# A fused two-block transformer layer on one core: inverse roots in 9 operations, half-empty weight tiles split only where they hold columns, and the compression blocks of the keys built earlier

## The reference

```python
# every norm of both blocks
y = xf * lax.rsqrt(jnp.mean(xf * xf, axis=-1, keepdims=True) + eps)

# second block: one projection gives everything
hn = rms_norm_2(h, attn_pre_norm)
proj = hn @ w_in
(q_n, k_c, v_c, k_s, v_s, k_w, v_w, g_n, q_w, k_sw, v_sw) = jnp.split(proj, IN_SPLITS, axis=-1)
# widths: q_n 512, six of 128, g_n 24, q_w 512, k_sw 128, v_sw 128

def compress(kv, pe, w1, w2):                 # for keys and for values
    ch = kv.reshape(B, S // 16, 16, H, D)
    blocks = jnp.concatenate([ch[:, :-1], ch[:, 1:]], axis=2) + pe[None, None, :, None, :]
    flat = blocks.transpose(0, 1, 3, 2, 4).reshape(B, nc, H, 32 * D)
    return jax.nn.gelu(flat @ w1) @ w2        # nc = 15 blocks, H = 2 heads, D = 64

# then: compressed, selected and windowed attention, mixed by sigmoid(g_n), and beside them
# a sliding-window attention (q_w, k_sw, v_sw) with sinks; both normed and projected by w_out
```

## Time and profile before

| | us |
|---|---|
| median of 3 runs | 1259.17 (1258.34 to 1260.98) |
| the profiled execution | 1257.46 |
| its span, first to last instruction | 1255.7 |
| TensorE busy | 1185.2 (94%) |
| VectorE busy | 904.7 (72%) |
| ScalarE busy | 606.6 (48%) |
| DMA | 197.51 MB, mean 157 GB/s |
| mean granted TensorE clock | 0.978 of 2.4 GHz |

### The profile page before, as it was taken

How to read it: one execution, slowest core, us unless ns; L and a number is a source line. 1 busy time by engine, 2 the same in 40 slices (tenths; PEclk the granted TensorE clock), 3 DMA queues, 4 the chain that set the end, 5 groups by cost and what they waited for, 6 DMA issues and landing times.

```text
span 1255.7 us, 24116 instructions
## 1 busy us (share of the span) xinstructions
PE 1185.2 (94%) x9174; PEld 1128.2 (90%) x9174; DVE 904.7 (72%) x1532; ACT 606.6 (48%) x1032; POOL 69.0 (5%) x56
## 2 busy tenths in 40 slices
PE   8999999999999999998999999999978897999996
PEld 8988898999999999778899999999966597999996
DVE  6999876676666596556757666557887658999855
ACT  5754654544445434344444444544455634665541
POOL 1576000000000000000000000000000000000000
PEclk9999999999999999999999999999988997999998
DMA  7454342445555556125415455555642013454552
GB/s 272 169 181 154 135 168 101 139 168 197 170 195 171 201 179 229 45 70 177 169 60 196 170 187 181 201 181 192 215 143 101 35 34 105 168 196 167 200 203 67
DMA packets 32456, 197.51 MB, mean 157 GB/s; under 512 B 3712, under 2 KB 7936, under 8 KB 9472
## 3 DMA queue, kind: packets, MB, share of 16 engines
q1 hardware_dynamic: 30752, 194.14, 44.9%
q10 hardware_dynamic: 1632, 2.36, 0.5%
HBM read 193.08 MB, written 1.05 MB: 155 GB/s over the span
## 4 chain that ended last, share of the span: by engine, by line
PE 78%; DVE 14%; ACT 4%; issue 3%; DMA 1%; ACTq 0%; DVEq 0%; SPq 0%
PE acc L486 20%; PE acc L488 20%; PE acc L487 20%; PE acc L522 7%; DVE wlo L1393 3%; DVE wlo L1386 2%; PE acc L502 2%; PE acc L787 2%; ACT whi L984 1%; PE sc L751 1%; PE st L635 1%; DMA raw<-weights 1%; DVE mx L1734 1%; PE tp L776 1%; PE tp L486 1%
## 5 line engine op out<-in xcount | busy, mean ns | idle before, releaser
L486 PE MATMUL acc<-Hhi,whi 128*128 128x256 f32 x1376 | 391.6, 285 | 3.6 <-DVE wlo L1393 3.4
L487 PE MATMUL acc<-Hlo,whi 128*128 128x256 f32 x1376 | 389.3, 283 | 0.0
L488 PE MATMUL acc<-Hhi,wlo 128*128 128x256 f32 x1376 | 389.3, 283 | 0.0
L984 ACT ACTIVATE whi<-raw 128x1024 fp32r<-128x1024 f32 x161 | 170.0, 1056 | 338.6 <-PE acc L488 312.3
L1386 DVE TENSOR_TENSOR wlo<-raw,whi 128x1024 fp32r<-128x1024 f32 x162 | 199.9, 1234 | 106.9 <-ACT whi L984 104.4
L486 PEld LDWEIGHTS acc<-Hhi,whi 128*128 128x128 f32 x1376 | 264.1, 192 | 5.0 <-DVE wlo L1393 2.3
L487 PEld LDWEIGHTS acc<-Hlo,whi 128*128 128x128 f32 x1376 | 264.1, 192 | 0.2
L488 PEld LDWEIGHTS acc<-Hhi,wlo 128*128 128x128 f32 x1376 | 264.1, 192 | 0.0
L486 PE MATMUL acc<-FH,whi 128*128 128x256 f32 x784 | 223.0, 284 | 8.3 <-DVE wlo L1393 4.5
L488 PE MATMUL acc<-FH,wlo 128*128 128x256 f32 x784 | 220.7, 281 | 0.0
L1393 DVE TENSOR_TENSOR wlo<-raw,whi 128x1024 fp32r<-128x1024 f32 x162 | 200.2, 1236 | 1.3
(11 more groups left out here) (336 smaller groups left out, 1853.4 us busy)
## 6 DMA issues: line engine op xcount, KB each, us to landing
raw<-weights SPq DMA_DIRECT2D x177, 1024.0 KB, 4.9
MEM<-mem_in SPq DMA_DIRECT2D x2, 1024.0 KB, 7.5
held<-weights SPq DMA_DIRECT2D x2, 1024.0 KB, 5.8
E<-A ACTq DMA_DIRECT2D x14, 128.0 KB, 2.3
X<-x_in SPq DMA_DIRECT2D x4, 256.0 KB, 3.5
raw<-weights SPq DMA_DIRECT2D x2, 512.0 KB, 8.1
out<-X SPq DMA_DIRECT2D x4, 256.0 KB, 2.1
cst<-consts SPq DMA_DIRECT2D x1, 998.0 KB, 12.4
```

The costliest lines, as they stand in the source:

```text
L486: pe.matmul(dst, w, x, start=first, stop=False)
L487: pe.matmul(dst, w, xl, start=False, stop=False)
L488: return pe.matmul(dst, wl, x, start=False, stop=last)
L984: act.activation(whi[j][:, 0:HALF, :], raw[j][:, 0:HALF, :], ACT.Copy).then_inc(hi_out, 1)
```

## The change

Three things. First, `inverse_root` takes 9 operations: mean plus eps as before; one multiply-add on the bits, read and written as integers; one Newton-like step with other constants; and one step of third order, as four operations. The buffer `nwi` goes. Second, `SWA_KEYS` and `SWA_VALUES` name the two tiles with zero columns: ScalarE and VectorE split only the first 128 and 152 columns of each chunk, TensorE makes only output half m = 0 of the first and products with 152 moving columns for the second, and copy, partners and rotation of the keys are one chunk wide. Third, the blocks of the keys are built ahead of rotation 6 and tile 7's product, on VectorE and ScalarE; `window_rest(0)` moves ahead of `ahead("win", 0, 8, 7)` and the values; TensorE's wait ahead of the attention is taken out, and the first `hidden_part` waits for one result fewer.

```diff
+GUESS_SLOPE, GUESS_TOP = 0.703952253, 0.703952253 * 2.38924456
+CUBIC_SCALE = 0.375 ** 0.5
...
+SWA_KEYS, SWA_VALUES = T0["win"] + 6, T0["winv"]
+WIDTHS = {SWA_KEYS: P, SWA_VALUES: P + 24}
...
+        def rot_chunks(name, k):
+            return 1 if T0[name] + k == SWA_KEYS else 2
...
                     if turned:
-                        mm = three(dst, x[:, o], xl[:, o], w, wl, a, z)
+                        n = slice(0, width)
+                        mm = three(dst[:, n], x[:, o], xl[:, o], w[:, n], wl[:, n], a, z)
...
-                turns = NTILES[name] // 2
+                turns = NTILES[name] // 2 - (name == "win")
...
             stage("win", Hhi, Hlo, source="down1", norm_name="pre2")
+            tile_in(L0["win"] + 6)
+            pe.wait_ge(acc_free, G0["win"] + 7)
+            columns(0, Hhi, Hlo, 0).then_inc(tile_done, 1)
+            tile_in(L0["win"] + 7)
+            pe.wait_ge(acc_free, G0["win"] + 8)
+            for m in range(2):
+                mm = columns(1, Hhi, Hlo, m)
+            mm.then_inc(tile_done, 1)
             to_tokens("pre2")
             tile_in(L0["winv"])
             pe.wait_ge(acc_free, G0["winv"] + 1)
             for m in range(2):
-                mm = columns(0, Hhi, Hlo, m, turned=True)
+                mm = columns(0, Hhi, Hlo, m, turned=True, width=WIDTHS[SWA_VALUES])
...
                     if kv:
                         pe.wait_ge(mix_out, 1)
+                    else:
+                        pe.wait_ge(acc_free, G0["win"] + 8 + 2)
...
-            pe.wait_ge(acc_free, G0["attn_nsa"] + 2)
             attention("attn_nsa", {5: turn_hidden, 7: compressed, 8: lambda: pe.wait_ge(cmp_ready, 1),
...
-                act.activation(whi[j][:, 0:HALF, :], raw[j][:, 0:HALF, :], ACT.Copy).then_inc(hi_out, 1)
+                act.activation(whi[j][:, 0:HALF, 0:width], raw[j][:, 0:HALF, 0:width], ACT.Copy).then_inc(hi_out, 1)
...
                     for j in range(2):
+                        if name == "win" and 2 * i + j == 7:
+                            window_blocks(0)
...
-                ins = dve.tensor_tensor(out=wlo[j][:, 0:HALF, :], in0=raw[j][:, 0:HALF, :], in1=f(whi[j][:, 0:HALF, :]),
+                ins = dve.tensor_tensor(out=wlo[j][:, 0:HALF, n], in0=raw[j][:, 0:HALF, n], in1=f(whi[j][:, 0:HALF, n]),
                                         op=ALU.subtract)
...
-                link(dve.tensor_scalar(nwi[:, 0:n], v.bitcast(I32), 1, None, op0=ALU.logical_shift_right))
-                link(dve.tensor_scalar(y.bitcast(I32), nwi[:, 0:n], -1, 0x5F3759DF, op0=ALU.mult, op1=ALU.add))
-                for step in range(3):
-                    link(dve.scalar_tensor_tensor(out=a, in0=y, scalar=-0.5, in1=v, op0=ALU.mult, op1=ALU.mult))
-                    link(dve.tensor_tensor(out=a, in0=a, in1=y, op=ALU.mult))
-                    ins = dve.scalar_tensor_tensor(out=y if step < 2 else dst, in0=a, scalar=1.5, in1=y, op0=ALU.add, op1=ALU.mult)
...
+                link(dve.tensor_scalar(y.bitcast(I32), v.bitcast(I32), -0.5, float(0x5F1FFFF9), op0=ALU.mult, op1=ALU.add))
+                link(dve.scalar_tensor_tensor(out=a, in0=y, scalar=-GUESS_SLOPE, in1=v, op0=ALU.mult, op1=ALU.mult))
+                link(dve.tensor_tensor(out=a, in0=a, in1=y, op=ALU.mult))
+                link(dve.scalar_tensor_tensor(out=y, in0=a, scalar=GUESS_TOP, in1=y, op0=ALU.add, op1=ALU.mult))
+                if between:
+                    between()
+                link(dve.scalar_tensor_tensor(out=a, in0=y, scalar=CUBIC_SCALE, in1=v, op0=ALU.mult, op1=ALU.mult))
+                link(dve.tensor_tensor(out=a, in0=a, in1=y, op=ALU.mult))
+                link(dve.scalar_tensor_tensor(out=a, in0=a, scalar=-1.25 / CUBIC_SCALE, in1=a, op0=ALU.add, op1=ALU.mult))
+                return dve.scalar_tensor_tensor(out=dst, in0=a, scalar=1.875, in1=y, op0=ALU.add, op1=ALU.mult)
...
             rotate("win", 5)
-            rotate("win", 6)
-            tile("win", 0, 8, 7)
-            dve.wait_ge(acc_free, G0["win"] + 7 + 2)
-            out_acc(dve.tensor_tensor(out=A[:, VC_SLOT:VC_SLOT + 2, :], in0=acc[1][:, :, :], in1=both(R[:, :]), op=ALU.mult))
...
             window_blocks(0)
+            rotate("win", 6)
+            tile("win", 0, 8, 7)
+            dve.wait_ge(acc_free, G0["win"] + 7 + 2)
+            out_acc(dve.tensor_tensor(out=A[:, VC_SLOT:VC_SLOT + 2, :], in0=acc[1][:, :, :], in1=both(R[:, :]), op=ALU.mult))
+            window_rest(0)
             ahead("win", 0, 8, 7)
             to_tokens("pre2")
             tile("winv", 0, 1, 0)
             out_acc(values_out(1, acc[0]))
-            window_rest(0)
```

More of the change, by code:

```diff
@@ L189, in build @@
         nw = sb("nw", [P, 3, S])
-        nwi = sb("nwi", [P, S], I32)
         mx, nb, rs = (sb(n, [P, 2, 4]) for n in ("mx", "nb", "rs"))
@@ L524, in whole, with columns @@
                 mm.then_inc(tile_done, 1)
-            def columns(j, xhi, xlo, m, ks=range(KC), turned=False, first=True, last=True, to=None):
+            def columns(j, xhi, xlo, m, ks=range(KC), turned=False, first=True, last=True, to=None, width=MB):
                 o = slice(m * P, (m + 1) * P)
@@ L976, in _, with split @@
             ac = Chain(act, act_chain)
-            def split(load, j, done=None, between=None):
+            def split(load, j, done=None, between=None, width=MB):
                 act.wait_ge(raw_loaded[j], load)
@@ L1001, in ahead @@
                 if not last and not (isinstance(i, int) and per * i + t + 2 in WHOLE_TILES):
-                    split(16 * (per // 2) * i + 16 * (t // 2 + 2), (T0[name] + k) % 2, per * i + (t + 1), between)
+                    split(16 * (per // 2) * i + 16 * (t // 2 + 2), (T0[name] + k) % 2, per * i + (t + 1), between,
+                          WIDTHS.get(t + 2, MB) if isinstance(i, int) and i == 0 else MB)
             def acc_out(name, g):
@@ L1076, in partners @@
                 for half in range(2):
-                    act.dma_start(E[half::every, n % 3, :, :], A[1 - half::every, at:at + 2, :]).then_inc(partner_in[n % 3], 16)
+                    act.dma_start(E[half::every, n % 3, 0:chunks, :], A[1 - half::every, at:at + chunks, :])\
+                        .then_inc(partner_in[n % 3], 16)
             def late_keys(k):
@@ L1325, in ready_chunks @@
                         act.activation(pair(SQ, 2 * p), pair(src, 2 * p), ACT.Square).then_inc(s_sq, 1)
-            plain("win")
             def window_blocks(kv):
@@ L1332, in window_blocks @@
                 act.activation(FHf[:, 2 * kv * 480:(2 * kv + 1) * 480], ZT, ACT.Copy).then_inc(s_taken, 1)
-            window_blocks(0)
+            plain("win")
             acc_out("winv", 0)
@@ L1382, in _, with lower @@
             f = lambda ap: ap.bitcast(F32)
-            def lower(j, after, between=None, head=False):
+            def lower(j, after, between=None, head=False, width=MB):
+                n = slice(0, width)
                 dve.wait_ge(hi_out, after + (-1))
-                ins = dve.tensor_tensor(out=wlo[j][:, 0:HALF, :], in0=raw[j][:, 0:HALF, :], in1=f(whi[j][:, 0:HALF, :]),
+                ins = dve.tensor_tensor(out=wlo[j][:, 0:HALF, n], in0=raw[j][:, 0:HALF, n], in1=f(whi[j][:, 0:HALF, n]),
                                         op=ALU.subtract)
@@ L1392, in lower @@
                 dve.wait_ge(hi_out, after)
-                dve.tensor_tensor(out=wlo[j][:, HALF:KC, :], in0=raw[j][:, HALF:KC, :], in1=f(whi[j][:, HALF:KC, :]),
+                dve.tensor_tensor(out=wlo[j][:, HALF:KC, n], in0=raw[j][:, HALF:KC, n], in1=f(whi[j][:, HALF:KC, n]),
                                   op=ALU.subtract).then_inc(lo_dve, 1)
@@ L1408, in ahead @@
                 if not last and not (isinstance(i, int) and per * i + t in WHOLE_TILES):
-                    lower((T0[name] + k) % 2, 2 * per * i + 2 * (split_before(t) + 1), between)
+                    lower((T0[name] + k) % 2, 2 * per * i + 2 * (split_before(t) + 1), between,
+                          width=WIDTHS.get(t, MB) if isinstance(i, int) and i == 0 else MB)
             def tile(name, i, per, k):
@@ L1446, in inverse_root @@
                     link(dve.tensor_scalar(v, v, eps, None, op0=ALU.add))
[L1447 to L1459 removed]
+                link(dve.tensor_scalar(y.bitcast(I32), v.bitcast(I32), -0.5, float(0x5F1FFFF9), op0=ALU.mult, op1=ALU.add))
[8 more added lines that the diff above has]
+                return dve.scalar_tensor_tensor(out=dst, in0=a, scalar=1.875, in1=y, op0=ALU.add, op1=ALU.mult)
+            NORM_LINKS = 1 + 3 + 4
             def norm(name, between=None, eps=RMS_EPS):
@@ L1560, in rotate @@
             def rotate(name, k):
-                n, at = ROT0[name] + k, ROT_SLOT[name] + 2 * k
-                q, partner = A[:, at:at + 2, :], E[:, n % 3, :, :]
+                n, at, chunks = ROT0[name] + k, ROT_SLOT[name] + 2 * k, rot_chunks(name, k)
+                q, partner = A[:, at:at + chunks, :], E[:, n % 3, 0:chunks, :]
```

(7 more changed lines are left out.)

14 lines of the change are left out of this document (4 added, 10 removed).

## The result

| | before | after |
|---|---|---|
| profiled execution, us (span) | 1257.46 (1255.7) | 1249.37 (1247.5) |
| median, us | 1258.36 | 1250.52 (6 runs, 1248.87 to 1251.98) |
| ratio, 95% interval | | 0.9934 [0.9919, 0.9949] |

The kernel became 7.8 us faster, where the forecast had 6.85. Two more sets of six runs of after gave ratios of 0.993 [0.9916, 0.9944] and 0.9946 [0.9931, 0.9962]. Over its 18 runs the mean span is 1249.0 us, over 92 runs of before 1256.6: 7.6 us. Two further runs of before, 1644.81 and 1916.14 us long at granted clocks of 0.65 and 0.555, are in no mean and no ratio here.

A forecast was written before the change was run, and what follows sets the result against it. VectorE was taken as the chain from 894 to 932 us, TensorE nearly everywhere else. Roots 2.35 plus narrow tiles and order 4.5 gave 6.85 us: 1259.17 to 1252.3 us, likeliest 1251.3 to 1253.2, range 1250.2 to 1256.7.

The forecast's parts named there:

- mix0: The shorter root there ends TensorE's wait for tile 3's `wlo`; gain 0.69 us, bounds 0.3 to 0.8.
- ffn0, ffn1: The shorter root removes a stall at tile 3's start in each of these stages; 0.24 us each.
- post2 and fpost2: Two TensorE waits on VectorE's `rt` columns, at the end of a root, shrink by 0.59 us each.
- final, pre2, the others: Shorter roots there gain nothing, as VectorE then waits for ScalarE's splits or the root ends early; others at most 0.1 each.
- Tile 6: Sliding keys in win: narrower split and low parts bring 1.5 us; VectorE's wait at tile 7 costs 0.2.
- The idle time before `wlo` 8: VectorE's 1.38 us idle before winv's low parts goes, as tile 6 ends earlier; +1.4 us, with 0.7 of cover.
- `wlo` 8 and the last rotation: VectorE in win: winv's narrower low parts save 0.8 us (0 to 1.1), the half-wide last rotation 0.8.
- Scores: TensorE no longer waits for the values ahead of the scores, so VectorE's 0.39 us wait goes; +0.4 us.
- gates: ScalarE's gates wait for the values with tile 10's split behind them, so VectorE gets `wlo` 10 late; -0.35 us.
- Rival 2: Tile 8's load lands after 7 us, not 4.9; 1.4 us come back and 0.6 at tile 9; 1254.3 us, chance 0.10.
- Narrow products: Winv's products with 152 moving columns take 0.12 us each, bounds 0.116 to 0.257; removing columns brings TensorE nothing.
- Rivals 3 and 4: Winv's products cost 0.257 us each (1256.3 us, chance 0.10) or 0.43, off the one-pass path (1264.8 us, 0.03).

The follow-up runs named there:

- e9: Before with idle TensorE products in waits: 7 before win's statistics, 9 before the third compression part, 5 before and 11 behind post2's root broadcast; 1256.76 us, ratio 0.9986.
- e14: Before with the narrow tiles alone, keeping the old root and old order; 1254.55 us, ratio 0.9965 to before.
- e3: After with the old inverse root put back, so narrow tiles and new order alone; 1254.03 us, ratio 0.9969 to before.
- e6: After with ScalarE's splits of tiles 6 and 8 made as narrow as VectorE's low parts; 1248.94 us, ratio 0.9926 to before.
- e15: After with both tiles in full, so new roots and new order without narrow tiles; 1255.36 us, ratio 0.9973 to before.
- e10: After with idle TensorE products in waits before win's statistics, before the third compression part (9) and around post2's root broadcast; 1252.51 us, ratio 0.995 to before.
- e7: After with winv split, multiplied and copied out in all 256 columns again; 1251.62 us, ratio 0.994 to before.
- e8: After with idle TensorE products in four waits, 16 of them before the third compression part; 1249.47 us, ratio 0.9936 to before.

## Why the prediction was right or wrong

The forecast was 1252.3 us, the result 1250.52. That lies in the full range (1250.2 to 1256.7), but 0.8 us below the likeliest case (1251.3 to 1253.2). Of the 1.8 us between forecast and result 0.8 are the starting point (a median of three runs, 1259.17, where the later ones gave 1258.4); the gain was 1.0 larger than forecast.

Two steps failed. The first is a cost: that a ScalarE half of tile 6 goes from 1.06 to about 0.6 us. It stayed at 1.05, so tile 6 gave 0.72 us where 1.5 - 0.2 was forecast. The second is a term put at nothing without a reason: the forecast took the clock of the one trace of before for both kernels, and let it change, for the worse, in the third part alone. The runs show after at the higher mean clock (0.9767 for 0.9750), worth about 1.3 us in its favour. The errors have opposite signs, so the nearness of 6.85 to 7.8 us is in part luck; the changed places by themselves gave 6.5. By the steps, each against the column or row that bears on it:

- **mix0**, 0.69 forecast: 0.83. The nearness is luck. The wait didn't go, as the sign of being right had it; it shrank by the whole root, 1.25 us, from 1.70 to 0.44, and 0.4 came back in the convolution. The 0.69 came from a trace in which tile 0 had run at 0.77 of the clock; e9 and e14, slow at the same place, show 0.67 and 0.70 with the old root.
- **ffn0, ffn1**, 0.24 each: 0.33 each. The stall was longer than the one gap between two starts; the tile ran through without any in after.
- **post2 and fpost2**, 0.59 each: the waits shrank by 0.6 each; the stretches show 0.2 to 0.5 and 0.65.
- **final, pre2, the others**, nothing: confirmed; tiles 0 to 5 of win have the same times in e3 and after.
- **Tile 6**, 1.5 less 0.2: 0.72, by the first failed step; e6, which makes the ScalarE half 0.62 us, gives 0.8 us more. Of TensorE's gap before the tile 0.35 us stayed.
- **The idle time before `wlo` 8**, 1.4: 1.45. Late next was the DMA, as I wrote. It landed at 898.9, and the first half of the split was done at 899.97, 0.1 us before VectorE came, where I had 0.7 us of cover. "Tile 8's split behind its DMA" stood among the signs of being wrong; it did wait for the DMA (1.43 us), and nothing was lost, as in the forecast's own account. Rival 2 (a landing after 7 us) did not occur.
- **`wlo` 8 and the last rotation**, 0.8 and 0.8: 0.71 and 0.77. **Values** 0.15: 0.22. **Scores** +0.4 and **gates** -0.35: +0.39 and -0.33, confirmed by e15.
- Their sum is 3.9 for 4.5 us, and 6.5 for 6.85 with the roots.
- **Narrow products**, 0.12: 0.111, a little under my lower bound of 0.116; 5.59 us for the tile. Rivals 3 and 4 fell. The tile ended 2.6 us before VectorE took it out. (The forecast says that the tile costs from an end at 918.7 on. By its own two us of cover it costs from about 914.2 on; at 918.7 the whole 4.5 us are gone, and rivals 3 and 4 are priced so.)
- **Clock** (rival 1), up to 1.5 lost in the third part: it took 4.5 us, as in the first trace of before, though its pause was 4.33 and not 3.73 us. The rest of the clock is the second failed step: I took one trace's clock for the kernel's own. The Trainium skill ("TensorE: Matmul & The Clock Gate", the part on the HAM clock gate) says that an idle array falls to half clock and that work releases it. The traces agree in part: 0.69 behind a wait of 1.9 us and 1.00 with idle products in it, but 4 of 13 traces did not fall there at all. And the fall can come when the array is already at work again: the third part of after starts at 926.31 at 1.00, and is at 0.50 from 926.80 on, as the windows below show; in e10 it came during the idle products.

```profile
926.30:926.60 0.30, 0.29 (x3) 0.28 (x4) 0.30 (x1) 0.00 (x0) 0.00 (x0) 1.00 1.03 437
926.80:929.80 3.00, 3.00 (x16) 2.38 (x15) 1.68 (x2) 0.00 (x0) 0.00 (x0) 0.50 0.52 153
```

- **The chances**: its own cases add up to 0.85 faster and 0.12 same, for the stated 0.87 and 0.10.

That the clock explains the last 1.3 us is inferred from spans at equal clock. The fit puts about two thirds of its rise with the roots; why shorter roots should raise it was not found.

## What to carry to other kernels

Where one helper serves two engines, check for each engine with which arguments it is called before pricing "the tile becomes narrow"; the operation's shape in the new trace shows it at once. Take at least two traces of the same code before reading a difference between two kernels, and align them by stretches: here a single stretch of unchanged code moved by up to 4.5 us. When a tile is shortened on an engine with time over it, look for the gain elsewhere: winv's narrow tile brought 1.0 us of VectorE's time and nothing on TensorE (e7). It is otherwise where another engine waits for the tile's end: the 1.45 us before `wlo` 8 are there because its split waits for tile 6 on TensorE. Idle products in a wait are worth up to 1.5 us at each place, but they have to end before it does (e8). The 7 that began with the wait held the clock in 5 of 5 traces; those that began behind an idle time of 1.5 to 2.4 us held it in 4 of 5.
